# Where a gated linear recurrence puts its score products in the matmul stream of TensorE

## The reference, cut to what matters

```python
proj = (u @ w_in).reshape(B, S, 4, H, K)
q_raw, f_raw, v, g = proj[:, :, 0], proj[:, :, 1], proj[:, :, 2], proj[:, :, 3]
log_f = log(lb + (1 - lb) * sigmoid(f_raw))
k = (1 - lb) * sigmoid(-f_raw);  q = silu(q_raw)
b = cumsum(log_f within a chunk)
q_dec, k_inv = q * exp(b), k * exp(-b)
a = where(causal, q_dec @ k_inv.T, 0)                  # the scores
o_intra = a @ v
k_end = k * exp(b_last - b);  chunk_decay = exp(b_last)
for each chunk:                                        # the states
    o_inter = q_c @ state
    state = chunk_decay[..., None] * state + k_end_c.T @ v_c
o = rms_norm(o_intra + o_inter) * norm_g * silu(g)
return o @ w_out
```

## Time and profile before

| what | value |
|---|---|
| median of 3 runs | 3810.97 us |
| the profiled execution | 3815.24 us |
| its span | 3813.4 us |
| mean granted TensorE clock | 0.964 |
| PE busy | 3550.7 us (93%) |
| VectorE busy | 1929.5 us (51%) |
| ScalarE busy | 1352.2 us (35%) |
| the recurrence | from about 2044 to 2326 us of the span |

### The profile page before, as it was taken

How to read it: one execution, slowest core, us unless ns; L and a number is a source line. 1 busy time by engine, 2 the same in 40 slices (tenths; PEclk the granted TensorE clock), 3 DMA queues, 4 the chain that set the end, 5 groups by cost and what they waited for, 6 DMA issues and landing times.

```text
span 3813.4 us, 43212 instructions
## 1 busy us (share of the span) xinstructions
PE 3550.7 (93%) x18038; PEld 2891.3 (76%) x18038; DVE 1929.5 (51%) x2633; ACT 1352.2 (35%) x1896; POOL 143.8 (4%) x108
## 2 busy tenths in 40 slices
PE   7899988999999999899997998999889999979998
PEld 2685557888888755688886777888778888778887
DVE  5436446777444444465545554433354545554333
ACT  3322343422323333353345445422343323353223
POOL 0000000000000000000000003100210000040001
PEclk9999998999999999999998999999999999989998
DMA  4431003444444230145532221233232323212321
GB/s 174 132 116 56 12 23 112 142 151 155 148 127 128 89 105 1 45 133 186 180 124 63 59 60 46 95 100 100 67 83 67 90 67 80 81 56 89 100 97 47
DMA packets 366625, 360.68 MB, mean 95 GB/s; under 512 B 65071, under 2 KB 312030, under 8 KB 365023
## 3 DMA queue, kind: packets, MB, share of 16 engines
q1 hardware_dynamic: 366211, 357.84, 30.5%
q10 hardware_dynamic: 220, 0.07, 0.0%
HBM read 350.02 MB, written 4.72 MB: 93 GB/s over the span
## 4 chain that ended last, share of the span: by engine, by line
PE 45%; ACT 5%; DVE 5%; issue 2%; POOL 1%; DMA 0%; SPq 0%; POOLq 0%; DVEq 0%; ACTq 0%
PE ps L402 39%; DVE second_w_lo L548 1%; ACT second_w_hi L489 1%; PE ps L2518 1%; DVE r_st L2412 1%; ACT second_scr L684 1%; PE ps L2539 1%; PE ps L2541 1%; PE ps L2291 1%; POOL sums L466 1%; POOL sq L463 1%; PE ps L2528 1%; DVE x_res L869 0%; PE ps L2268 0%; DVE second_scr L867 0%
## 5 line engine op out<-in xcount | busy, mean ns | idle before, releaser
L402 PE MATMUL ps<-second_h_hi,second_w_hi 128*128 128x512 f32 (+1 forms) x2216 | 832.9, 376 | 51.2 <-DVE second_h_lo L895 17.0
L402 PE MATMUL ps<-second_h_lo,second_w_hi 128*128 128x512 f32 (+1 forms) x2216 | 813.2, 367 | 0.0
L402 PE MATMUL ps<-second_h_hi,second_w_lo 128*128 128x512 f32 (+1 forms) x2216 | 812.8, 367 | 0.0
L548 DVE TENSOR_TENSOR second_w_lo<-ring,second_w_hi 128x2048 fp32r<-128x2048 f32 (+2 forms) x176 | 390.6, 2220 | 480.8 <-ACT second_w_hi L489 480.8
L402 PEld LDWEIGHTS ps<-second_h_hi,second_w_hi 128*128 128x128 f32 x2216 | 432.2, 195 | 119.7 <-issue 27.4
L402 PEld LDWEIGHTS ps<-second_h_lo,second_w_hi 128*128 128x128 f32 x2216 | 432.2, 195 | 63.5 <-issue 1.7
L402 PEld LDWEIGHTS ps<-second_h_hi,second_w_lo 128*128 128x128 f32 x2216 | 430.4, 194 | 65.4
L489 ACT ACTIVATE second_w_hi<-ring 128x2048 fp32r<-128x2048 f32 (+2 forms) x176 | 311.5, 1770 | 342.6 <-PE ps L402 334.7
L402 PE MATMUL ps<-h_mix_hi,w_hi 128*128 128x512 f32 (+3 forms) x776 | 274.3, 354 | 26.6 <-DVE h_mix_lo L711 18.7
L402 PE MATMUL ps<-h_mix_lo,w_hi 128*128 128x512 f32 (+3 forms) x776 | 271.1, 349 | 0.0
L402 PE MATMUL ps<-h_mix_hi,w_lo 128*128 128x512 f32 (+3 forms) x776 | 270.4, 349 | 0.0
(11 more groups left out here) (401 smaller groups left out, 5803.5 us busy)
## 6 DMA issues: line engine op xcount, KB each, us to landing
ring<-in_w_mlp SPq DMA_DIRECT2D x64, 1024.0 KB, 5.3
side_w<-in_ada_w SPq DMA_DIRECT2D x96, 512.0 KB, 4.3
ring<-in_ffn_w_in SPq DMA_DIRECT2D x44, 1024.0 KB, 5.1
side_w<-in_w_mod SPq DMA_DIRECT2D x80, 512.0 KB, 3.8
ring<-in_attn_w_in SPq DMA_DIRECT2D x48, 512.0 KB, 5.2
ring<-in_hgrn_w_in SPq DMA_DIRECT2D x32, 512.0 KB, 4.8
ring<-in_ffn_w_out SPq DMA_DIRECT2D x16, 1024.0 KB, 4.9
ring<-in_w_in SPq DMA_DIRECT2D x14, 1024.0 KB, 5.4
```

The source lines that it names most:

```text
L402: mm = pe.matmul(acc, lhsT, rhs, start=k == 0 and wp == ap, stop=k == j.kt - 1 and wp == 1)
L548: dve.tensor_tensor(unit.place(unit.slot[1]), unit.place(M.ring[:, u % RING, :]), unit.place(unit.slot[0]), ALU.subtract).then_inc(*S.w_lo ...
```

## The change

It moves three of the side thread's steps on TensorE, and two more by one K tile. Nothing is added or removed. The streams of VectorE, ScalarE, GpSimd and the DMA queue are the same row by row.

```diff
@@ RecurrenceThread.tensor
         tr.then_inc(*S["rec_turned"].one)
+        yield self.jobs[2].at + 0.15
+        R.wait_done(pe, self.jobs[2])
+        for t in range(4):
+            tr = pe.transpose(M.ps[:, 7, ...], B.vf[...], M.ident[:, :])
+        tr.then_inc(*S["rec_vturned"].one)
+        yield self.jobs[2].at + (0.4 if self.tail else 0.55)
         pe.wait_ge(S["rec_mul"].sem, S["rec_mul"].at(3 * n + 3))
         for t in range(4):
             c = slice(t * P, (t + 1) * P)
             mm = pe.matmul(M.ps[:, 4, c], B.nb[:, c], B.qs[:, c], start=True, stop=True)
         mm.then_inc(*S["rec_scores"].one)
-        yield self.jobs[2].at + 0.15
-        R.wait_done(pe, self.jobs[2])
-        for t in range(4):
-            tr = pe.transpose(M.ps[:, 7, ...], B.vf[...], M.ident[:, :])
-        tr.then_inc(*S["rec_vturned"].one)
-        yield self.jobs[2].at + 0.7
+        yield self.jobs[2].at + (0.7 if self.tail else 0.8)
         pe.wait_ge(S["rec_ket"].sem, S["rec_ket"].at(n + 1))
...
-        yield self.later(0.75, 0.25)
+        yield self.later(0.85, 0.25)
         pe.wait_ge(S["rec_state"].sem, S["rec_state"].at((self.N_CHUNKS - 1) * (n + 1)))
...
-        yield self.later(1, 0.4)
+        yield self.later(1.1, 0.4)
         pe.wait_ge(S["rec_sq"].sem, S["rec_sq"].at(n + 1))
```

More of the change, by code:

```diff
@@ L2264, in tensor @@
         tr.then_inc(*S["rec_turned"].one)
+        yield self.jobs[2].at + 0.15
+        R.wait_done(pe, self.jobs[2])
+        for t in range(4):
+            tr = pe.transpose(M.ps[:, 7, t * P:(t + 1) * P], B.vf[:, t * P:(t + 1) * P], M.ident[:, :])
+        tr.then_inc(*S["rec_vturned"].one)
+        yield self.jobs[2].at + (0.4 if self.tail else 0.55)
         pe.wait_ge(S["rec_mul"].sem, S["rec_mul"].at(3 * n + 3))
@@ L2269, in tensor @@
         mm.then_inc(*S["rec_scores"].one)
-        yield self.jobs[2].at + 0.15
-        R.wait_done(pe, self.jobs[2])
-        for t in range(4):
-            tr = pe.transpose(M.ps[:, 7, t * P:(t + 1) * P], B.vf[:, t * P:(t + 1) * P], M.ident[:, :])
-        tr.then_inc(*S["rec_vturned"].one)
-        yield self.jobs[2].at + 0.7
+        yield self.jobs[2].at + (0.7 if self.tail else 0.8)
         pe.wait_ge(S["rec_ket"].sem, S["rec_ket"].at(n + 1))
```

## The result

The changed kernel takes 3780.27 us (median of 4 runs, 3778.57 to 3784.44) and the kernel before 3811.7 us (4 runs: the three of the table and one more). The ratio is 0.9917, 95% interval 0.9900 to 0.9935: 31.4 us faster, where 30.4 us and a time of 3781 were forecast. What moves on TensorE, by the diff, are four steps: the scores by five K tiles (four in the last head), and state products, outputs and sum by one each in the heads before the last; the value transposes keep their place among the gate matmuls.

A forecast was written before the change was run, and what follows sets the result against it. TensorE, 93% busy, was taken as the bound, mainly by its scores' 25.5 us wait for the scaled query. Waiting 23.6 plus clock 6.8 gave 30.4 us off 3810.97, so 3781 us, range 3771 to 3795.

The forecast's parts named there:

- the clock: Low-clock stretches behind TensorE's idle time before the scores go: 6.8 us gained, bounds 0 and 11.1.
- heads 2 to 7: The scores no longer wait for the scaled query in these heads: 2.6 us gained each, 15.6 in all.
- Head 0: Value transposes newly wait 2.5 us for ScalarE, scores wait 0.6; work moved ahead of the scores gains 4.0 us.
- Head 1: Scores still wait 0.2 us for the query; work moved ahead of them gains 4.0 us.
- VectorE is free by then: At the masked scores, VectorE makes the mask 0.5 us before the state products need it: cost 0.
- The first rival: Waits go but the clock gives nothing, or takes some back behind the outputs: 3787 to 3795 us, chance 0.20.
- half a fall: Head 0 keeps a 2.5 us wait, so half its 2.4 us low-clock loss behind the scores counts as gained: 1.2.
- the falls behind the outputs: Low clock from outputs to sum in heads 1 and 4, 3.1 us in all, counted as gained only in the upper bound.
- the forecast with all terms: All waiting and clock gains arrive: 3774 to 3786 us, chance 0.66.
- The second rival: The wait moves to state products (mask) or outputs (states): 3811 us, or 3800 if half is lost; chance 0.08.
- the third: Slower: clock falls at the scores and stays low to the sum, 10.0 us a head, 3837 in five heads; chance 0.04.
- the fourth: VectorE's low part moves too, so the scores' wait stays: 3811 us, chance 0.02.

The follow-up runs named there:

- Head 0 too: Scores behind 12 and state products behind 18 gate matmuls in all heads, plus head 0's weight conversion behind the query on ScalarE and VectorE: 3782.06 us.
- the wait filled: Kernel before, its order kept, with discarded matmuls (8 in head 0, 4 in head 1, 3 in others) ahead of the scores' wait: 3807.55 us against 3814.24.
- The outputs' wait: Changed kernel with scores behind 12 and state products behind 18 gate matmuls in all heads, outputs and sum unmoved: 3781.24 us, ratio 0.9914 to the kernel before.
- The changed kernel again: The changed kernel timed and profiled again without any edit: 3783.38 us against 3813.66 for the kernel before, ratio 0.9918.
- The scores' move alone: Changed kernel with only the scores at their new place; state products, outputs and sum where they were before: 3782.42 us, ratio 0.9916 to the kernel before.
- Scores close to the state products: Changed kernel with the scores behind 18 gate matmuls, 3 ahead of the state products (last head unchanged): 3783.49 us against 3814.56 for the kernel before.
- Less cover: Changed kernel with the scores directly behind the value transposes, 6 gate matmuls ahead instead of 15: 3792.97 us against 3814.56 for the kernel before.
- the later steps alone: Kernel before with only state products, outputs and sum moved by one K tile, scores unmoved: 3813.14 us against 3814.56, ratio 0.9999.

## Why the prediction was right

*The sum.* 30.4 us were forecast, 31.4 measured, and 30.3 when it was timed again. The terms are less exact than their sum: waiting came 0.8 us short and the clock gave more in the first pair of profiles, so two errors have opposite signs, and the runs of one kernel spread over 5 us. That the number is within a microsecond is luck; the mechanism and its largest term, heads 2 to 7, are not.

*Heads 2 to 7.* Forecast 2.6 us each, 15.6. The timelines give 2.61 to 2.76 at equal clock, 16.0 in all. The prediction puts the scores 2.40 us behind the start of the key transposes in one place; 2133.01 less 2130.02 is 2.99, and 2.40 counts from the transposes' end. Its working uses the two times and is not touched by it.

*Head 0.* Forecast 4.0, found 3.85. The new waits are where they were said to be: 2.41 us for the values and 0.39 for the query. That cover counts by its length was also shown with less of it. The reason given for the long wait, that the query's chain starts with nothing ahead of it, is not what the trace of before shows. Head 0's exponentials end 0.2 us behind the start of its key transposes (in head 2 they end 4.9 us ahead of it), and then come a weight conversion and the load of a function table on ScalarE, and the low part on VectorE:

```profile
2051.16 1.90 ACT L489 ACTIVATE second_w_hi<-ring 128x2048 fp32r<-128x2048 f32 x1
2053.08 1.28 ACT L2320 ACT_TABLE_LOAD   x1
2054.37 0.60 ACT L2320 ACTIVATE r_qs<-ps 128x512 f32<-128x512 f32 x1
...
2055.68 2.28 DVE L548 TENSOR_TENSOR second_w_lo<-ring,second_w_hi 128x2048 fp32r<-128x2048 f32 x1
```

The forecast took the moment of 2058.61 from the trace and didn't need the reason; moving both weight operations gave the 2 us of "Head 0 too".

*Head 1.* Forecast 4.0, found 2.95. This is the step that failed in part: "VectorE is free by then" holds for heads 2 to 7 only. In head 1 a second group of four residual operations stands between the scaled query and the value copy, and the mask comes late (VectorE and TensorE of head 1, after):

```profile
2088.62 1.67 DVE L795 SCALAR_TENSOR_TENSOR x_res<-x_res,vec,sums 128x256 f32<-128x256 f32 x4
2090.21 0.69 DVE L2401 COPY sq<-ps 128x512 f32<-128x512 f32 x1
2090.81 0.68 DVE L2403 SCALAR_TENSOR_TENSOR sq<-ps,causal 128x512 f32<-128x512 f32 x1
...
2091.64 1.17 PE L2283 MATMUL ps<-sq 32*128 32x128 f32 x30 [0.92 <-DVE sq L2403]
```

It was in the trace of before, behind the scaled query (2094.99) and one more operation:

```profile
2096.19 1.67 DVE L795 SCALAR_TENSOR_TENSOR x_res<-x_res,vec,sums 128x256 f32<-128x256 f32 x4
```

I had read VectorE's queue up to the scaled query in head 1, and beyond it in head 2 only. It cost 0.9 us. The 0.2 us that the scores were to wait in head 1 are there: they start 4.59 us behind the key transposes, and 4.33 in heads 2 to 6.

*The clock.* Forecast 6.8, found 9.6 in this pair of profiles, some 2 us less with the profile of the changed kernel timed again, and 6.5 (3 to 10) by the timed runs with the wait filled. The first rival, that the clock gives nothing, falls by that run. The falls behind the scores are all gone in the profile. For head 0 half a fall was counted, because it keeps a wait of 2.4 us: behind that wait the clock stayed at 1.00 in two profiles (this one and "The outputs' wait") and was low in three (0.69, 0.69 and 0.65 up to the scores, in "The changed kernel again", "The scores' move alone" and "Scores close to the state products"); in "Less cover" a second wait follows. Of the falls behind the outputs I had assumed no change; two went and one came, which I put down to chance: the changed kernel's second profile has two, as many as the kernel before. The Trainium skill, "TensorE: Matmul & The Clock Gate", in "HAM oscillation — how this bites in real kernels", has each burst begin slowly when waits stand between the bursts; its example has waits of 3 to 5 us. The traces agree in part: the filled wait shows that the idle time is the cause, but waits of 2.4 us were followed by a fall in some heads and not in others. It doesn't explain the falls behind the outputs, which have no wait of more than 0.53 us ahead of them, and in two profiles none.

*The rest.* Outputs still wait 3.7 us in seven heads, the sum and the weights cost nothing, as forecast. Of the 36.2 us between the two spans 32.4 lie in the recurrence; 1.3 lie ahead of it and 2.5 behind it, where nothing was changed, and the spread of a kernel's own runs covers them.

One bound is not what its terms give: 23.6 + 11.1 us would lead to 3776, not 3774, as the lower end of the forecast with all terms. The second rival (the wait turns up elsewhere) is true of 1 us; the third (a low clock from scores to sum) was seen in no profile; the fourth falls by the list of waits.

What stays open is what lowers the clock behind the outputs. In ten of the twelve profiles it came in one to three of heads 0 to 6, in different heads, with and without waits at the scores and at the outputs; in two it didn't come. No run took away the outputs' short matmuls to test them.

## What to carry to other kernels

When an in-order engine waits at one step for an operand that is ready at a fixed moment, put as much independent work ahead of that step as the wait is long, measured in lengths from the timeline, and then check the next consumer by the same ruler: here 0.57 us were left, and 0.7 more would have moved the wait on. Read the other engine's queue in every iteration that differs, the first ones above all, up to the last operation that the moved step feeds. On TensorE a wait costs more than its length, since the clock may be low behind it: here 22.8 us less waiting made the kernel 30 to 31 us faster.

## What the runs showed of the hardware that I had not expected

Waits of one length don't cost the same: of the waits of 2.40 to 2.46 us ahead of the scores in heads 2 to 6, two of five in one profile (the kernel before) and four of five in another (the later steps alone) were followed by a stretch at the low clock, each costing 1.5 to 1.6 us; in heads 0 and 1 of the same profiles, behind 4.0 to 6.9 us, all four were. Behind waits of 0.6 us or less ahead of the scores none was seen. Filling the wait with discarded matmuls was 6.5 us faster than idling. And a 128x512 matmul of plain float32 operands is recorded as two passes of 0.43 us, 0.86 in all, against 0.23 us for one of the split projection operands. Last, a low clock can be hidden in part: behind both heads with slow outputs in the profile of "Less cover" the next head didn't wait for the query, where the others waited 0.6 us.
